# The first load of each weight casts straight into its ring slot, and the slot is written to the bf16 copy in HBM

## The reference, cut to what matters

```
for i in range(DEPTH):                                # DEPTH = 2, x: (16, 2048, 1024) f32
    h = rmsnorm(x, g_pre_mix[i])
    proj = h @ w_in_ret[j]  or  h @ w_in_fox[j]       # q | k | v | gate or forget logits | memory q
    self_out = retention(q, k, v) * silu(gate)  or  forgetting_attention(q, k, v, log_f)
    mem_out = memory_attention(mq, mem, g_mem[i], w_mem_kv[i])
    x = x + rmsnorm(concatenate([self_out, mem_out]) @ w_out[i], g_post_mix[i])
    h = rmsnorm(x, g_pre_mlp[i])
    u = relu(h @ w_up[i])                             # 1024 -> 4096
    x = x + rmsnorm((u * u) @ w_down[i], g_post_mlp[i])
```

## Time and profile before

| | |
|---|---|
| median of 3 runs | 3770.0 us (3764.7 to 3815.3) |
| the profiled execution | 3771.5 us |
| its span on the slowest core (core 4) | 3769.5 us |
| spans of the eight cores | 3721.4 to 3769.5 us |
| TensorE (PE) busy | 3328.8 us, 88% |
| VectorE (DVE) busy | 1942.9 us, 52% |
| ScalarE (ACT) busy | 1772.6 us, 47% |
| GpSimd (POOL) busy | 546.4 us, 14% |
| moved by DMA | 623.3 MB |

### The profile page before, as it was taken

One profiled execution on the slowest core, in us unless ns is written; L12 is line 12 of the kernel. 1 busy time (PEld: TensorE's weight loads), 2 busy tenths in 40 slices (PEclk: granted clock), 3 DMA queues, 4 the chain that ended last, 5 costly groups with the idle time before them and its releaser, 6 DMA issues.

```text
span 3769.5 us, 57487 instructions; the slowest of 8 cores (3721.4 to 3769.5 us)
## 1 busy us (share of the span) xinstructions
PE 3328.8 (88%) x16476; PEld 1542.9 (41%) x16476; DVE 1942.9 (52%) x3273; ACT 1772.6 (47%) x3173; POOL 546.4 (14%) x518
## 2 busy tenths in 40 slices
PE   2546886898999977899999999999999989999996
PEld 1212432444444433444444444444444434444442
DVE  2454664655654342442676567666664454434414
ACT  2333443434573236577444444444447348585221
POOL 0211121111110110100231222122010110001102
PEclk8778998999999998999999999999999999999998
DMA  9999499649745687523655365535563463534535
GB/s 163 160 188 167 156 226 179 200 150 217 191 132 167 157 187 157 184 88 113 206 192 186 115 218 183 189 115 194 157 204 121 159 190 118 179 108 128 185 113 173
DMA packets 270386, 623.26 MB, mean 165 GB/s; under 512 B 54400, under 2 KB 66304, under 8 KB 270080
## 3 DMA queue, kind: packets, MB, share of 16 engines
q1 hardware_dynamic: 243680, 567.41, 49.1%
q0 software_dynamic: 26400, 52.17, 11.5%
HBM read 555.15 MB, written 168.56 MB: 192 GB/s over the span
## 4 chain that ended last, share of the span: by engine, by line
PE 68%; DMA 16%; DVE 6%; issue 4%; ACT 3%; SPq 2%; POOL 1%; DVEq 0%; ACTq 0%; POOLq 0%
PE pb L613 68%; DMA xt_s<-xT 3%; DMA vcache<-un_s 2%; SPq L648 2%; DMA xt_s<-xs 2%; DMA wm_s<-wbf 2%; DVE tb_s L636 1%; DVE un_s L633 1%; DMA wf_s<-wbf 1%; DMA un_s<-kcache 1%; DMA mkv_s<-memkv 1%; DMA xt_s<-memT 1%; DVE un_s L652 1%; DVE xt_s L633 1%; DMA wbf<-wall 1%
## 5 line engine op out<-in xcount | busy, mean ns | idle before, releaser
L613 PE MATMUL pb<-hb_s,wf_s 128*128 128x512 bf16 x4096 | 983.6, 385 | 83.6 <-DMA wf_s<-wbf 37.7
L613 PE MATMUL pb<-u_s,wf_s 128*128 128x512 bf16 x4096 | 999.6, 382 | 21.4 <-DMA wf_s<-wbf 8.3
L613 PE MATMUL pb<-hb_s,wm_s 128*128 128x512 bf16 (+1 forms) x2240 | 587.7, 388 | 49.8 <-DMA wm_s<-wbf 38.8
L613 PEld LDWEIGHTS pb<-hb_s,wf_s 128*128 128x128 bf16 x4096 | 399.2, 99 | 563.8 <-issue 130.9
L624 ACT ACTIVATE pt_s<-pb,dcol_s 128x512 bf16<-128x512 f32 x960 | 560.3, 623 | 141.0 <-PE pb L613 129.8
L613 PEld LDWEIGHTS pb<-u_s,wf_s 128*128 128x128 bf16 x4096 | 396.9, 98 | 474.9 <-issue 47.1
L633 DVE TENSOR_TENSOR u_s<-rb_s 128x512 bf16<-128x512 bf16 x512 | 246.3, 482 | 537.3 <-ACT rb_s L624 536.2
L624 ACT ACTIVATE rb_s<-pb 128x512 bf16<-128x512 f32 x512 | 303.7, 594 | 447.7 <-PE pb L613 364.1
L613 PE MATMUL pb<-un_s 65*128 65x512 bf16 (+5 forms) x1536 | 411.1, 307 | 39.8 <-DMA un_s<-kcache 30.5
L624 ACT ACTIVATE sq_s<-xt_s 128x512 bf16<-128x512 f32 (+1 forms) x400 | 238.7, 609 | 414.9 <-DVE xt_s L633 268.8
L613 PE MATMUL pb<-pt_s,un_s 128*128 128x512 bf16 x960 | 331.6, 348 | 0.1
(11 more groups left out here) (68 smaller groups left out, 2615.4 us busy)
## 6 DMA issues: line engine op xcount, KB each, us to landing
wf_s<-wbf SPq DMA_DIRECT2D x288, 512.0 KB, 4.5
wm_s<-wbf SPq DMA_DIRECT2D x152, 768.0 KB, 6.2
xs<-xt_s SPq DMA_DIRECT2D x192, 256.0 KB, 6.1
xt_s<-xs SPq DMA_DIRECT2D x192, 256.0 KB, 6.9
xt_s<-xT SPq DMA_DIRECT2D x128, 256.0 KB, 8.3
wbf<-wall POOLq DMA_DIRECT2D x32, 1024.0 KB, 26.0
y<-xt_s SPq DMA_DIRECT2D x112, 256.0 KB, 4.0
xt_s<-y SPq DMA_DIRECT2D x112, 256.0 KB, 4.9
```

What stands on the lines that cost most here:

```text
L613: S.add("pe", lambda e: e.matmul(out, lhsT=lhsT, rhs=rhs, start=start, stop=stop, **kw), reads=reads, writes=writes, cost=c)
```

## The change

A key's first use no longer loads from `wbf`. A DMA on POOL's queue reads the f32 units from `wall` and casts them into the ring slot itself. When the planner is done with that use (`done`), SP writes the slot to `wbf`, and every later use loads from there as before. The memory keys `mkv` are cast in both of their uses. `caster`, its groups and its lead are gone, and with them all casts from HBM to HBM. The MLP ring's loads start only when the core of stage 0 is planned to be done. The planner's costs of DMAs change with it (a unit's cast from 2300 to 1840 ns, plain bytes from 280 to 300 per ns), which can move the order of other work.

```
-            if keys[0][1] == layers[0] and i >= 3:
-                p_ = rs_[i - 3]
-                yield lambda: o < used[0] + LEAD // 2 or S.avail["pe"] >= p_.last_w.end - 2000.0
-            else:
-                yield lambda: o < used[0] + LEAD
...
-            S.add("pool", (...)(rows(DR["wbf"], o, n), DR["wall"][o * 128:(o + n) * 128, 0:1024]),
-                  reads=after, writes=[r_], dma=True, ncast=n)
...
+    def casts(key):
+        return 2 if key[0] == "mkv" else 1
...
             while self.issued < len(self.plan):
                 i = self.issued
                 key = self.plan[i]
-                yield lambda: i < self.released + self.n and gR[key].last_w is not None
                 slot = i % self.n
                 o, n = wall_idx[key]
-                dst = self.tile[:, slot, 0:n, :].rearrange("p a b -> p (a b)")
-                yield ("sp", [gR[key]], [self.R[slot]])
-                spdma(dst, flat(DR["wbf"], o, n), [gR[key]], [self.R[slot]], self.R[slot], n * 262144)
+                u = uses.get(key, 0)
+                direct = u < casts(key)
+                yield lambda: i < self.released + self.n and (direct or key in wbR)
+                uses[key] = u + 1
+                if direct:
+                    src = DR["wall"][o * 128:(o + n) * 128, 0:1024].rearrange("(p j) f -> p j f", p=128)
+                    yield ("pool", [], [self.R[slot]])
+                    S.add("pool", (...)(self.tile[:, slot, 0:n, :], src),
+                          writes=[self.R[slot]], dma=True, ncast=n)
+                    self.back[i] = u == casts(key) - 1
+                else:
+                    src = DR["wbf"][o * 131072:(o + n) * 131072].rearrange("(p f) -> p f", p=128)
+                    yield ("sp", [wbR[key]], [self.R[slot]])
+                    spdma(..., src, [wbR[key]], [self.R[slot]], self.H[slot], n * 262144)
                 self.issued += 1
...
         def done(self, *keys):
             for k in keys:
+                i = self.open[k]
+                if self.back.get(i):
...
+                    spdma(DR["wbf"][...], self.tile[:, slot, 0:n, :].rearrange("p a b -> p (a b)"),
+                          [self.R[slot]], [wbR[k], q], q, n * 262144)
...
-            K.spawn(caster(), 0)
...
-    K.spawn(WF.loads(), 0)
+    K.spawn(WF.loads(wait("core", 0, 0, 0)), 0)
```

More of the change, by code:

```diff
@@ L26 @@
 WPAD = 16
-LEAD = 24
 SLACK = 700.0
@@ L72, in __init__ @@
         self.wire = 0.0
-        self.cwire = 0.0
         self.ops = []
@@ L156, in add @@
         op.end = t + cost
[L157 to L162, removed]
+        if dma:
+            self.wire = max(t + 1500, self.wire) + (ncast * 1840.0 if ncast else nbytes / 300.0)
+            op.end = self.wire + 400.0
         self.avail[eng] = t + (1000.0 if ncast else 60.0) if dma else op.end
@@ L524, in schedule @@
     X = {it: {} for it in items}
[L527 to L534, removed]
-        else:
[L536 to L552, removed]
-            if keys[0][1] == layers[0] and i >= 3:
-                p_ = rs_[i - 3]
-                yield lambda: o < used[0] + LEAD // 2 or S.avail["pe"] >= p_.last_w.end - 2000.0
-            else:
-                yield lambda: o < used[0] + LEAD
[L558 to L562, removed]
-                  reads=after, writes=[r_], dma=True, ncast=n)
-            rs_.append(r_)
-            ev("cast", keys[-1])
+    wbR = {}
+    uses = {}
+    qR = [Res(f"wb{i}") for i in range(6)]
+    nq = [0]
+    def casts(key):
+        return 2 if key[0] == "mkv" else 1
     class WRing:
@@ L572, in __init__ @@
             self.R = [Res(f"{name}{i}") for i in range(n)]
+            self.H = [Res(f"{name}h{i}") for i in range(n)]
             self.order = []
@@ L577, in __init__, with loads @@
             self.open = {}
-        def loads(self):
+            self.back = {}
+        def loads(self, start=None):
             if self.plan is None:
                 return
+            if start:
+                yield start
             while self.issued < len(self.plan):
@@ L584, in loads @@
                 key = self.plan[i]
-                yield lambda: i < self.released + self.n and gR[key].last_w is not None
                 slot = i % self.n
                 o, n = wall_idx[key]
-                dst = self.tile[:, slot, 0:n, :].rearrange("p a b -> p (a b)")
-                yield ("sp", [gR[key]], [self.R[slot]])
-                spdma(dst, flat(DR["wbf"], o, n), [gR[key]], [self.R[slot]], self.R[slot], n * 262144)
+                u = uses.get(key, 0)
[5 more added lines that the diff above has]
+                    yield ("pool", [], [self.R[slot]])
+                    S.add("pool", (lambda d_, s_: lambda e, sem: e.dma_start(out=d_, in_=s_).then_inc(sem, 16))(self.tile[:, slot, 0:n, :], src),
+                          writes=[self.R[slot]], dma=True, ncast=n)
[3 more added lines that the diff above has]
+                    yield ("sp", [wbR[key]], [self.R[slot]])
+                    spdma(self.tile[:, slot, 0:n, :].rearrange("p a b -> p (a b)"), src, [wbR[key]], [self.R[slot]], self.H[slot], n * 262144)
                 self.issued += 1
@@ L601, in take @@
             slot = i % self.n
-            used[0] = max(used[0], sum(wall_idx[key]))
             return [self.tile[:, slot, j, :].rearrange("p (k m) -> p k m", k=8) for j in range(wall_idx[key][1])], self.R[slot], slot
@@ L606, in done @@
             for k in keys:
+                i = self.open[k]
+                if self.back.get(i):
+                    slot = i % self.n
+                    o, n = wall_idx[k]
+                    wbR[k] = Res("")
+                    q = qR[nq[0] % len(qR)]
+                    nq[0] += 1
+                    spdma(DR["wbf"][o * 131072:(o + n) * 131072].rearrange("(p f) -> p f", p=128), self.tile[:, slot, 0:n, :].rearrange("p a b -> p (a b)"),
+                          [self.R[slot]], [wbR[k], q], q, n * 262144)
                 del self.open[k]
@@ L818, in first_norm @@
         if i == 0:
-            X[(s, b)]["x0"] = list(xs)
-            K.spawn(caster(), 0)
             K.spawn(rotary(s, b), 1)
```

## The result

The changed kernel took 3616.3 us (median of four runs, 3609.1 to 3651.0), the kernel before in the same comparison 3767.6 us (3764.7 to 3815.3): a ratio of 0.959 with a 95% interval of 0.949 to 0.969. The profiled execution of after took 3619.1 us with a span of 3617.4, that of before 3771.5 with 3769.5: 152 us less in both.

What follows compares the result with a forecast made beforehand. It took full DMA engines, with casts running ahead of need and in bursts, to leave TensorE idle. Terms -60 - 17 + 0 - 28 + 10 - 34 + 6 = -123 us took 3771.5 to 3648, or 3647 us as median; range 3585 to 3755.

Steps and rivals of the forecast that it cites:

- Stage 0, -60: 0 to 240 us: no casts ahead of need, less DMA work, ending near 180 us; -60 us (-30 to -68).
- the two ways to the number: Stage 0: DMA work falls from 230 to 162 us, or TensorE's two waits on DMAs go, leaving 172 us.
- 240 to 300: Behind stage 0: TensorE's wait for the next block's norm shrinks as casts leave the DMA engines; -17 us (0 to -30).
- MLP 0: 300 to 600 us, with stages 1 and 2: layer 0's MLP units all cast here; 0 us (-21 to +9).
- 600 to 700: The burst of layer 1's mixer casts goes; -28 us of 40 us of idle (0 to -37).
- 850 to 1000, +10: Stage 4, first of layer 1, now casts its 29 units itself; +10 us (0 to +26).
- The hole at 1275 and layer 1's MLP, -34 + 6: Layer 1's first MLP job: casts ahead go, -34 us (0 to -45); keys through three slots, +6 (0 to +79).
- cast's price, 2.0 us a unit: Assumed time of a unit's cast into SBUF, between bounds of 1.71 (plain f32 load) and 2.18 us (cast before).
- A cheaper cast: Rival: HBM traffic sets a cast's price, so a unit costs 1.45 us; -155 or so, 3615 us; chance 0.18.
- The lead was worth it: Rival: without casts ahead, work collides with its own use; -20 us, 3750, no change to be told; chance 0.22.
- The slot's cycle: Rival: slow casts and writes bind MLP 0's slots, from a 28 us cycle on; +90, 3860 us; chance 0.10.
- signs of being wrong: Next profile: `wf_s<-wall` waits of 20 us per ten keys, stage 4 waits on `wm_s<-wall`, or writes landing after slot use.

Runs made afterwards that it cites:

- e_l0: Changed kernel with only layer 0's first loads cast straight to slots, layer 1's keys cast in HBM ahead as before: 0.993 of the kernel before.
- e_none: Changed kernel's code and planner costs, but every key cast in HBM ahead and the MLP ring loading from the start, as before: 1.010 of the kernel before.
- e_l1: Changed kernel with only layer 1's first loads cast straight to slots, layer 0's keys cast in HBM ahead as before: 0.983 of the kernel before.
- e_lead: Kernel before, with layer 0's casts kept within 12 units of the last weight used, still inside HBM: 3752 us, 1.001 of the kernel before.
- e_via: Changed kernel with keys cast at the same points but into the HBM copy, then loaded to the slot, no write back: 0.991 of the kernel before.
- e_x: Changed kernel with the second and third weight casts held until the fifth tile of the first x block landed: 0.959 of the kernel before.
- e_via3: As e_via, but each key cast when the slot three keys ahead of its own comes free: 0.992 of the kernel before.

## Why the prediction was right, and where it was not

3647 us with a range of 3585 to 3755, faster: 3616 lies in it. By its own steps, in the order of the sum:

- *Stage 0, -60:* -57.8. The end near 180 us is there (181.1), and e_l0 shows that layer 0's direct casts make it (180.1) while e_none and e_l1 stay at 262. One of the two ways to the number holds: the waits for `wm_s` and the memory keys go, from 68.4 to 8.5 us. The reason given, less DMA work because no unit is cast ahead of need, was the smaller part. Fewer units in the stretch, still cast inside HBM, give 22 us (e_lead) or 14 (e_via); by the medians of the eight cores these are 18 and 10 of 52. In e_via the DMA time up to the end of stage 0 is 152 us, below the 162 of the forecast, and TensorE still waits 40.4 us there for `wm_s` and the memory keys. The larger part comes only when the first use does not go through HBM, for which the prediction had no term; that the number came out so near is in part luck. The DMA time was priced too high: 162 us for 38 units, measured 139 (76.8% of 181.1) for 44. What bounds the stage now is the other chains, as the 180 assumed; the start of x is one, with 8 to 12 us (e_x).
- *240 to 300, MLP 0, 600 to 700: -17, 0 and -28, together -45.* Measured -93 from the end of stage 0 to that of stage 2, or about -65 without the MLP work that moved. The -17 for the norm of the next block came in part: in the 61 us behind stage 0 the idle time falls by 10.4 us, and a wait of 17.5 us for the squares of x is still there. The burst of layer 1 at 600 is confirmed by e_l1. The mis-sized term is **MLP 0 at 0**: I held the stretch for DMA's as well as TensorE's, with casts at 2.0 us. In after's 300 to 600 us the units took 1.74 us, the DMA share is 0.85, and TensorE has no wait for `wf_s` against 21.0 us. The expectation of a share above 0.9 until 550 us was wrong with it: 0.77, 0.75 and 0.88.
- *850 to 1000, +10:* from the end of stage 2 to that of stage 4, +5.7.
- *The hole at 1275 and layer 1's MLP, -34 + 6:* from stage 4's end to stage 6's -5.5, and about -33 without the 28 us of MLP work that comes back there. The hole is gone in e_l1 as well.
- *The sum:* -123 against -152. About -20 of the difference are MLP 0 and what lies beside it, the rest is spread over the others with 2 to 5 us each. With the first goes the **cast's price, 2.0 us a unit, measured 1.73**, at the low bound of 1.71 and not near the cast of before; for the 68 units of that stretch this is 18 us of DMA time. How much of the -20 it makes no run shows; the 21.0 us of waits for `wf_s` that went are as large.

The rivals. *A cheaper cast* gave 3615 us, but by a price of 1.45 us that no run shows; it came to the right time with a wrong number. The Trainium skill's page "DMA: Bandwidth & Descriptors" (Bandwidth), by which HBM traffic binds, led to an estimate of 1.46 us into SBUF and 2.20 inside HBM. Here the first is 1.73, and the second 1.91 in e_via (380 us for 199 units), where before had 2.18: the first and e_via do not agree with it, and the measurement decides. *The lead was worth it* falls: with direct casts the lead is gone and stages 1 and 2 gain most. *The slot's cycle* did not bind: cast and write of an MLP slot take 8.6 and 7.6 us, where 28 us for the cycle would decide, and over the whole span TensorE waits 12.9 us for `wf_s<-wall`. Two of the signs of being wrong did show, without harm: TensorE waits 7.4 us for `wm_s<-wall` in stage 4, and casts do wait for their slot's write. What POOL waited for in after over the span:

```profile
POOL wf_s L562 <- DMA wbf<-wf_s: 95.7, 19, 17.1
```

What stays open: how much of e_via's 117 us is the two steps' length, how much the dearer cast and the greater traffic inside HBM, how much SP's queue standing behind the casts, and how much the planner's other order of work. e_via3 was to separate the first and brought the crowd back instead.

## What to carry to other kernels

When work ahead of need fills the DMA engines, look at its way before its timing: here holding it back only moved the hole (e_lead), and a first use through HBM lost either by its two steps (e_via) or by its crowd (e_via3), while casting into the slot and writing the copy off the path won 4%. Then look for what shares a queue: half of such a change was worth 1 or 2%, and in e_l0 the casts that remained stood ahead of the slots' casts on the same queue. And try to let the first operand that is computed on land before the bulk of the weights: the first projection started 8.4 us earlier here, for some 0.3% of the run, not clear of noise.

## What the runs showed of the hardware that I had not expected

- A cast from f32 into SBUF costs about what the f32 bytes cost at the mean rate of the plain DMAs: 1.73 us per 512 KB read (some 303 GB/s) against 1.71 by q1's rate in before and 1.66 in after. No run has a plain read of the f32 weights.
- The price of a cast inside HBM is not fixed, and was higher in the more crowded runs: 2.18 us a unit over the span of before, 1.91 in e_via. In stage 0 alone it is 2.00 in e_via (36.4% of 224.9 us for 41 units) and 2.19 in e_via3 (41.8% of 228 for 43.6 units).
- POOL's casts look like one queue in order: with eight casts issued within 6 us among them, three slot casts took 14.1, 51.6 and 75.8 us to land in the order of issue, in place of 8.6. That the DMA engines were also full then is not separated from it.
- 172 us more of DMA time, spread over a span in which DMA is busy some 60%, cost 76 us, slots held longer and another order of work included.
